# Two of ten weighted row sums move from VectorE to ScalarE and TensorE in the last stage of a decoder layer

## Chip, core and metric

The kernel runs on one NeuronCore of a Trainium2 chip. The metric is the device time of one execution in microseconds (us); less is better. A core has five engines that run their own instruction streams and meet only at semaphores: TensorE (PE, matmuls, into the accumulator memory PSUM), VectorE (DVE), ScalarE (ACT), GpSimd (POOL, here above all the issuer of indirect DMAs) and SyncE (SP, the issuer of most other DMAs).

## The reference, cut to what matters

The reference computes one decoder layer for 512 prompt tokens and 8 sample tokens of width 1024: a mixer of two attention groups, a mixture of experts with two experts for each token, and a final norm. The change lies behind the last expert, in the sum over the two experts, the residual and the norm:

```python
combine = jnp.sum(jax.nn.one_hot(expert_id, N_EXPERTS) * (g_w * top_w)[..., None], axis=1)
act = jax.nn.silu(gate) * up * combine[..., None]
y = jnp.einsum('nef,efd->nd', act, w_down)
x = x + y
output = rms_norm(x, norm_final)
```

Each token has two nonzero weights in `combine`, so its `y` is (first weight x the row of its first choice) + (second weight x the row of its second choice).

## The kernel before, in words

**Tiles.** The 520 tokens are five tiles: tiles 0 to 3 have 128 prompt rows each, tile 4 (the sample rows) has 8. `x[:, i, :]` holds tile i in SBUF, 1024 float32 to a row.

**Experts.** Sixteen experts run one after the other; the program streams their weights from memory. An expert's result rows are stored to `expert_rows` (`y_dram`) in memory. The last two experts (numbers 14 and 15, `LATE = 14`) are not stored: their rows stay in SBUF as `y_late`, and TensorE distributes them with 0/weight matrices `late_pick` (built earlier) straight into PSUM.

**The final stage.** After the stores have landed, POOL gathers, for each tile in the order `SUM_ORDER = (0, 4, 1, 2, 3)`, the two rows of each token from `expert_rows` (L2351, ten indirect DMAs). A tile then goes through these steps:

1. TensorE opens its two PSUM banks with zeros (`open_banks`, a bf16 product with zero weights, L2698). Tiles 0 and 4 are opened before the last down projection, tiles 1 and 2 right after it. Tile 3 uses tile 0's banks, and so is opened once tile 0 has been read for the last time.
2. VectorE, `add_rows(i)`: L2673 adds first weight x first rows to `x`; L2677 writes second weight x second rows + `x` into the banks.
3. TensorE adds the rows of the late experts with four matmuls of 64 rows by 512 columns (L2914), two on array rows 0 to 63 and two on 64 to 127.
4. ScalarE squares and sums the banks (L2452), then takes the inverse root by Ln and Exp (L2453, L2455).
5. VectorE, `scaled(i)`: L2683 multiplies the banks by that and by the gain, into `x`; SP stores `x` (L2309).

Each engine's order is written out by hand and is kept: VectorE does `add_rows` for 0, 4, 1, 2, then `scaled(0)`, `add_rows(3)`, then `scaled` for 4, 1, 2, 3. TensorE and ScalarE go through the tiles in `SUM_ORDER`. An `overflow` branch, ahead of the final stage on every engine, handles experts with more rows than were planned for; it is not entered with these inputs, but each engine loads a count and branches past it.

Of the kernel before, what the change touches and what calls it, by code (L numbers as in the profile page):

```python
# [16 lines left out]
ACT = mybir.ActivationFunctionType  # L17
# [19 lines left out]
TILES = QT + 1  # L37
# [30 lines left out]
FIRST = P + 2  # L68
SUM_ORDER = (0, 4, 1, 2, 3)
OPEN_FIRST = (0, 4)  # L70
CHUNKS = [("gate", 0), ("gate", 1), ("up", 0), ("up", 1), ("down", 0), ("down", 1), ("gate", 2), ("up", 2)]
CHUNKS += [("down", 2), ("gate", 3), ("up", 3)]
CHUNKS += [(w, j - (w == "down")) for j in range(4, 15) for w in ("gate", "up", "down")]
# [118 lines left out]
def body(nc, ctx, a, out, cf_at, cf_n, cb_at, cb_n):  # L192
# [1969 lines left out]
    for i in SUM_ORDER:  # L2162
        sg.mark(f"gathered{i}", i, 32)
        sg.mark("early", ("first", i))
        sg.mark("early", i)
    for i in OPEN_FIRST + (1, 2):
        sg.mark("late_full", ("open", i))
    for i in SUM_ORDER:
        if i == 2:
            sg.mark("late_full", ("open", 3))  # L2170
        sg.mark("late_full", i)
        sg.mark("ssq_final", i)
        sg.mark("final", i)
        sg.mark("st_y", i, 16)
    final_waits = [(n, t) for n, t in sg.total.items() if n.startswith("st_")]
# [68 lines left out]
    def expert_sync(sp, kind, key):  # L2244
        if kind == "expert0":
            sg.wait(sp, "x_full", ("vproj", LATE_VALUES[-1]))
            load_chunk(sp, 0, FIXED[0])
            load_chunk(sp, 1, FIXED[1])
        elif kind == "chunk":
            n, = key  # L2250
            if n == 3:
                sg.wait(sp, "z_full", sb_units[-1])
            elif n == 4:
                sg.wait(sp, "t_full", ("probT",) + turned[-1] + (1,))
            elif n == 2:
                sg.wait(sp, "pv", turned[-1])
                sp.wait_ge(sg["st_v"], sg.total["st_v"])
            elif n == 5:
                sg.wait(sp, "m_full", ("wout", QT - 1, 1))
            elif n == 6:  # L2260
                sg.wait(sp, "m_full", ("wout", QT - 1, 3))
            load_chunk(sp, n, FIXED[CHUNKS[n][1]])
        elif kind == "chunk_part":
            n, part = key
            if part == 0:
                sg.wait(sp, "squares", QT - 1)
                load_chunk(sp, n, FIXED[CHUNKS[n][1]], (slice(0, 4), slice(6, 8)))
            else:
                sp.wait_ge(sg["e_rowsT_full"], 2)
                sp.wait_ge(sg["st_h2"], sg.total["st_h2"])  # L2270
                load_chunk(sp, n, FIXED[CHUNKS[n][1]], (slice(4, 6),))
        elif kind == "experts":
            expert_reg = list(FIXED)

            def next_expert(j):

                expert_reg.append(sp.value_load(order_i[0:1, j:j + 1], min_val=0, max_val=NE - 1))

            for n in range(RING, len(CHUNKS)):
                before, j = USED[n - RING]  # L2280
                if CHUNKS[n] == ("gate", 3):
                    sg.wait(sp, "x_dve", ("order",))
                if CHUNKS[n][0] == "gate":
                    next_expert(CHUNKS[n][1])
                sp.wait_ge(sg["e_" + before], freed(j))
                load_chunk(sp, n, expert_reg[CHUNKS[n][1]])
                if CHUNKS[n] == ("gate", LATE - 1):
                    sg.wait(sp, "x_dve", ("idx",))
                    sg.wait(sp, "extra", 0)
                    sg.wait(sp, "y_slots", 0)  # L2290
                    sp.dma_start(gain[:, :], a["norm_final"].rearrange("(o d) -> o d", o=1).partition_broadcast(P).rearrange(
                        "p o d -> p (o d)")).then_inc(sg["gain_in"], 16)
            def more(v):
                e = sp.value_load(extra_i[0:1, bass.ds(v, 1)], min_val=0, max_val=NE - 1)
                row = sp.value_load(extra_i[0:1, bass.ds(v + EXTRA, 1)], min_val=0, max_val=NE * CAP - P)
                load_all(sp, e, sg["v_w"])
                sp.dma_start(more_f[:, :], table[bass.ds(row, P), :]).then_inc(sg["v_idx"], 16)
                sp.wait_ge(sg["v_y"], 2 * v + 2)
                sp.dma_start(y_dram[bass.ds(v * P + EXPERT_ROWS, P), :], y_more).then_inc(sg["v_st"], 16)
                sp.wait_ge(sg["v_st"], 16 * v + 16)  # L2300
                sp.sem_inc(sg["v_passed_sp"], 1)

            sp.wait_ge(sg["e_down"], finished(LAST))
            overflow(sp, more, lambda: sp.sem_inc(sg["v_all"], 1))
        elif kind == "final":
            for i in SUM_ORDER:
                sg.wait(sp, "final", i)
                dst = out["y_p"][0, i * P:(i + 1) * P, :] if i < QT else out["y_s"][:, 0, :]
                sp.dma_start(dst, x[0:ROWS[i], i, :]).then_inc(sg["st_y"], 16)  # L2309

    def expert_gps(pool, kind, key):
# [10 lines left out]
        elif kind == "experts":  # L2322
# [32 lines left out]
            def gather_more():  # L2355
                pool.wait_ge(sg["v_all"], 2)
                for i in range(TILES):
                    for k in range(2):
                        nc.gpsimd.indirect_dma_start(gathered_more[0:ROWS[i], 2 * i + k, :], None, y_dram,
                                                     bass.IndirectOffsetOnAxis(ap=more_slots[0:ROWS[i], i, k:k + 1], axis=0)  # L2360
                                                     ).then_inc(sg["v_gathered"], 16)

            pool.wait_ge(sg["e_rowsT_full"], 2 * LAST)
            overflow(pool, more, gather_more)
    def expert_act(act, link, inverse_rms, kind, key):
# [10 lines left out]
        elif kind == "experts":  # L2376
# [68 lines left out]
                A.copy(y_more[:, 0:512], bank[2][:, :]).then_inc(sg["v_y"], 1)  # L2445
            overflow(act, more)
        elif kind == "final":
            for i in SUM_ORDER:
                r = ROWS[i]
                junk = work[0:r, 2048:3072].rearrange("p (a b) -> p a b", a=2)  # L2450
                sg.wait(act, "late_full", i)
                link(A.activation(junk, final_banks(i), ACT.Square, accum_out=small[0:r, 16 + i:17 + i]))  # L2452
                link(A.activation(small[0:r, 16 + i:17 + i], small[0:r, 16 + i:17 + i], ACT.Ln, bias=c["eps"][0:r],  # L2453
                                  scale=1.0 / D))
                A.activation(small[0:r, 16 + i:17 + i], small[0:r, 16 + i:17 + i], ACT.Exp, scale=-0.5  # L2455
                             ).then_inc(sg["ssq_final"], 1)

    def expert_dve(dve, link, kind, key):
        V = nc.vector
# [26 lines left out]
        elif kind == "experts":  # L2486
# [85 lines left out]
            def add_more():  # L2572
                dve.wait_ge(sg["v_gathered"], 32 * TILES)
                for i in range(TILES):
                    r, xi = ROWS[i], x[0:ROWS[i], i, :]
                    for k in range(2):
                        link(V.scalar_tensor_tensor(xi, gathered_more[0:r, 2 * i + k, :], weight[0:r, i, k:k + 1], xi,
                                                    ALU.mult, ALU.add))
                V.memset(smi[:, 40:41], 0).then_inc(sg["v_added"], 1)

            def y_out(j):
                if UNITS[j] <= 64:
# [86 lines left out]
        elif kind == "final":  # L2669
            def add_rows(i):  # L2670
                r, xi, to = ROWS[i], x[0:ROWS[i], i, :], final_banks(i)
                sg.wait(dve, f"gathered{i}", i)
                V.scalar_tensor_tensor(xi, gathered_rows(i, 0), weight[0:r, i, 0:1], xi, ALU.mult, ALU.add  # L2673
                                       ).then_inc(sg["early"], 1)
                sg.wait(dve, "early", ("first", i))
                sg.wait(dve, "late_full", ("open", i))
                V.scalar_tensor_tensor(to, gathered_rows(i, 1).rearrange("p (a b) -> p a b", a=2), weight[0:r, i, 1:2],  # L2677
                                       xi.rearrange("p (a b) -> p a b", a=2), ALU.mult, ALU.add).then_inc(sg["early"], 1)

            def scaled(i):  # L2680
                r = ROWS[i]
                sg.wait(dve, "ssq_final", i)
                V.scalar_tensor_tensor(x[0:r, i, :].rearrange("p (a b) -> p a b", a=2), final_banks(i), small[0:r, 16 + i:17 + i],  # L2683
                                       gain[0:r, :].rearrange("p (a b) -> p a b", a=2), ALU.mult, ALU.mult
                                       ).then_inc(sg["final"], 1)

            for i in (0, QT, 1, 2):
                add_rows(i)
            sg.wait(dve, "gain_in", "final")
            scaled(0)  # L2690
            add_rows(3)
            for i in (QT, 1, 2, 3):
                scaled(i)
# [21 lines left out]
    def expert_pe(pe, kind, key):  # L2715
# [186 lines left out]
        elif kind == "final":  # L2902
# [3 lines left out]
            for i in SUM_ORDER:  # L2906
                to = final_banks(i)
                if i == 2:
                    sg.wait(pe, "final", 0)
                    open_banks(3).then_inc(sg["late_full"], 1)  # L2910
                sg.wait(pe, "early", i)
                for q in range(2):
                    for h in range(2):
                        ins = T.matmul(to[:, h, :], late_pick(q, i)[64 * h:64 * h + 64, :], y_late[q][64 * h:64 * h + 64, :],  # L2914
# [368 lines left out]
```

## Time and profile before

| | us |
|---|---|
| median of 3 runs | 756.84 (755.36 to 759.11) |
| profiled execution, own time | 751.01 |
| its span | 749.2 |
| TensorE busy in the span | 697.4 (93%) |
| VectorE busy | 343.3 (46%) |
| ScalarE busy | 216.3 (29%) |
| first indirect gather of the final stage issued | 719.05 |
| end of VectorE's last instruction (744.78 + 1.28) | 746.06 |

The span is what the profiler saw of one execution; the execution's own time is 1.8 us more. The runs that make the median were timed without the profiler and are 0.6 to 1.1% above the profiled one. Times of instructions are counted from the span's start. An engine's busy share over the whole span says little about the last 20 us, which is all that the change touches.

### The profile page before, as it was taken

Reading aid. Unit: us, or ns where it says so; the run is one execution under the profiler, and the core shown is the slowest. Engines: PE = TensorE matmul, PEld = TensorE weight load, DVE = VectorE, ACT = ScalarE, POOL = GpSimd, SP = SyncE. Lnnn points to the kernel's source line nnn. Section 1 sums busy time; section 2 is a strip of 40 time slices with the busy share of each in tenths; the row PEclk is TensorE's granted clock in tenths of the full one; section 3 lists DMA queues with packets and bytes.
Section 4 is the critical chain, followed back from the end, with each engine's and each line's share of the span. In section 5 each row is a group of like instructions: output and inputs, shape, how many; then the busy total and the mean of one; then the engine's idle time right before and its main releaser. Section 6 shows DMA issues by size and latency. Waiting matters only on the chain.

```text
span 749.2 us, 13606 instructions
## 1 busy us (share of the span) xinstructions
PE 697.4 (93%) x5261; PEld 382.9 (51%) x5261; DVE 343.3 (46%) x770; ACT 216.3 (29%) x557; POOL 125.5 (17%) x174
## 2 busy tenths in 40 slices
PE   7978999999999989989979999989899999999985
PEld 3445456444554444545545564744465565566531
DVE  6422103595222465664784665523823543322238
ACT  1111111112321555757757852001101101101114
POOL 0111000120000443252242242110100000000040
PEclk9999999999999999989999999999999999999999
DMA  8266890677658530000000059999999999999995
GB/s 278 88 179 179 250 387 24 239 239 234 210 170 219 217 145 1 1 4 1 1 29 1 6 190 372 305 379 400 363 363 375 399 408 397 396 401 400 413 348 206
DMA packets 101523, 172.55 MB, mean 230 GB/s; under 512 B 22925, under 2 KB 40685, under 8 KB 101426
## 3 DMA queue, kind: packets, MB, share of 16 engines
q1 hardware_dynamic: 79714, 142.83, 53.6%
q10 hardware_dynamic: 18656, 20.35, 8.1%
q0 software_dynamic: 3088, 8.49, 3.2%
q8 instruction: 43, 0.70, 0.4%
q14 instruction: 22, 0.18, 0.1%
HBM read 151.78 MB, written 22.98 MB: 233 GB/s over the span
## 4 chain that ended last, share of the span: by engine, by line
PE 71%; DVE 7%; SPq 6%; issue 6%; ACT 4%; DMA 4%; POOL 0%; ACTq 0%; DVEq 0%
PE bank L2752 15%; PE bank L3242 13%; PE bank L2008 7%; PE bank L3225 6%; PE bank L2781 6%; SPq L1191 4%; PE bank L1946 3%; PE bank L1925 3%; PE bank L1804 2%; PE bank L2711 2%; PE bank L1959 2%; PE bank L2742 2%; DMA pages<-page_table 2%; PE bank L3246 1%; PE bank L2060 1%
## 5 line engine op out<-in xcount | busy, mean ns | idle before, releaser
L3242 PE MATMUL bank<-reg 128*128 128x512 f32 (+1 forms) x352 | 146.8, 562 | 1.2 <-DMA reg<-w_in 0.8
L2752 PE MATMUL bank<-reg,qreg 128*32 128x128 f32 (+2 forms) x1072 | 100.1, 340 | 0.9 <-ACT qreg L2380 0.6
L3242 PEld LDWEIGHTS bank<-reg 128*128 128x128 f32 x352 | 64.2, 191 | 59.4 <-issue 55.8
L2752 PEld LDWEIGHTS bank<-reg,qreg 128*32 128x32 f32 (+2 forms) x1072 | 59.3, 126 | 39.6 <-issue 25.1
L1290 POOL TENSOR_SCALAR reg<-reg,st,gates 128x128 f32<-128x128 f32 (+3 forms) x64 | 41.3, 655 | 181.9 <-DVE st L1578 181.8
L3225 PE MATMUL bank<-cf,reg 128*128 128x128 f32 (+1 forms) x384 | 61.4, 278 | 9.4 <-DVE rt L1769 4.9
L2008 PE MATMUL bank<-reg 128*128 128x512 f32 x128 | 65.0, 632 | 0.4 <-DVE x L1690 0.3
L3225 PEld LDWEIGHTS bank<-cf,reg 128*128 128x128 f32 (+1 forms) x384 | 41.6, 141 | 29.3 <-issue 24.5
L3076 ACT ACTIVATE work<-bank 128x128 f32<-128x128 f32 (+5 forms) x107 | 40.8, 411 | 49.0 <-PE bank L3225 47.7
L1574 DVE TENSOR_REDUCE st<-bank 128x2 f32<-128x256 f32 (+3 forms) x32 | 26.3, 823 | 44.8 <-PE bank L1927 44.7
L2781 PE MATMUL bank<-reg,work 128*32 128x256 f32 (+1 forms) x336 | 44.2, 475 | 1.8 <-ACT work L2391 1.6
L3180 DVE COPY work<-bank 128x128 f32<-128x128 f32 (+4 forms) x55 | 22.8, 429 | 50.4 <-PE bank L3225 50.3
L2330 POOL DMA_INDIRECT work<-h_rows,ids x14 | 13.6, 969 | 180.7 <-PE bank L2800 128.0
L1405 ACT ACTIVATE reg<-bank,st 128x128 f32<-128x128 f32 (+3 forms) x64 | 33.2, 525 | 27.4 <-DVE st L1574 27.1
L3043 POOL TENSOR_TENSOR reg<-reg,cf 128x128 f32<-128x128 f32 (+5 forms) x30 | 15.4, 532 | 145.7 <-ACT reg L3133 135.1
L1946 PE MATMUL bank<-work,vreg 128*64 128x128 f32 x480 | 37.1, 284 | 2.0 <-DVE work L3180 2.0
L1946 PEld LDWEIGHTS bank<-work,vreg 128*64 128x64 f32 x480 | 25.4, 137 | 24.4 <-issue 21.9
L2498 DVE TENSOR_SCALAR work<-work 128x256 f32<-128x256 f32 (+3 forms) x16 | 5.4, 335 | 70.8 <-ACT work L2386 70.7
L2499 DVE RECIPROCAL work<-work 128x256 f32<-128x256 f32 (+3 forms) x16 | 36.0, 2253 | 0.6
L2008 PEld LDWEIGHTS bank<-reg 128*128 128x128 f32 x128 | 22.8, 199 | 17.0 <-issue 16.1
L2399 ACT COPY work<-bank 128x512 f32<-128x512 f32 (+1 forms) x16 | 9.0, 560 | 72.5 <-PE bank L2781 52.1
L3133 ACT COPY reg<-bank 128x512 f32<-128x512 f32 (+1 forms) x20 | 10.9, 547 | 62.4 <-PE bank L3242 62.4
(380 smaller groups left out, 944.5 us busy)
## 6 DMA issues: line engine op xcount, KB each, us to landing
reg<-w_down SPq DMA_DIRECT2D x13, 2048.0 KB, 19.6
reg<-w_gate SPq DMA_DIRECT2D x12, 2048.0 KB, 13.6
reg<-w_up SPq DMA_DIRECT2D x10, 2048.0 KB, 16.0
reg<-w_in ACTq DMA_DIRECT2D x16, 512.0 KB, 6.0
expert_rows<-vreg SPq DMA_DIRECT2D x14, 512.0 KB, 6.7
vreg<-w_up SPq DMA_DIRECT2D x3, 2048.0 KB, 12.8
reg<-cache_sb_k SPq DMA_DIRECT2D x16, 256.0 KB, 4.4
reg<-cache_sb_v SPq DMA_DIRECT2D x16, 256.0 KB, 4.1
```

What stands on the lines that cost most here:

```text
L1191: sp.dma_start(dst[64 * pg:64 * pg + 64, l], src[:, l]).then_inc(sg[f"pair{q % PAIRS}"], 16)
L1290: ins = G.tensor_scalar(prob, prob, w[:, e:e + 1], gate[:, e:e + 1], ALU.mult, ALU.mult)
L1405: nc.scalar.activation(prob_of(key, e)[:, 0:n], at(ring, key)[:, 0:n], ACT.Exp, bias=st[:, top:top + 1], accum_out=st[:, col:col + 1]).the ...
L1574: V.tensor_reduce(st[:, top:top + 2], psum[:, 2:4, 0:n], AX.X, ALU.max, negate=True).then_inc(sg["arg"], 1)
L1946: ins = T.matmul(to[64 * e:64 * e + 64, :], v, probT[:, turn_at[key] % 3, e, k * P:(k + 1) * P], start=(k == 0 and b != WIN), stop=(k == i ...
L2008: ins = T.matmul(at(ring, ("wout", i, group))[0:r, :], chunks_of(i)[:, part, 0:r], w_out[group // 2][:, k, 512 * half:512 * half + 512], s ...
L2499: link_loop(V.reciprocal(s_, s_), 3 * j + 2)
L2752: ins = T.matmul(to[rows, at_:at_ + w], rowsT[b][:, k, r0:r0 + n], w_[:, k, h * w:(h + 1) * w], start=(k == 0), stop=(k == KD - 1))
L2781: ins = T.matmul(to[rows, at_:at_ + w], actsT[j % 2][:, 4 * r0 // P + k % per, a0:a0 + n], w_[:, k, w * h:w * h + w], start=(k == 0), stop ...
L3076: ins = nc.scalar.activation(dst, src, ACT.Copy, scale=scale)
L3225: ins = nc.tensor.transpose(dst, src, ident[0:src.shape[0], 0:src.shape[0]])
L3242: ins = nc.tensor.matmul(at("m", ("proj", n))[:, 0:w], hT[:, k, i * P:(i + 1) * P], win[:, pos % 2, k, 0:w], start=(k == 0), stop=(k == KD ...
```

## The change

`ON_ACT = (4, 1)`: for the sample rows and for tile 1, VectorE's second instruction of `add_rows` is left out. In its place ScalarE, in a new function `second(i)`, writes second weight x second rows into the opened banks. `x` (with the first choice's rows added by VectorE, as before) is added by TensorE: two matmuls with the identity as the stationary operand and 512 columns of `x` as the moving one, ahead of the four with the late rows. ScalarE does `second(4)` ahead of its first square and `second(1)` behind tile 0's norm; TensorE waits for it through `ssq_final`. Inside the overflow branch, gathers are repeated and waits added; the branch is not entered.

```diff
+ON_ACT = (4, 1)
...
+            def second(i):
+                sg.wait(act, f"gathered{i}", i)
+                sg.wait(act, "late_full", ("open", i))
+                A.activation(final_banks(i), gathered_rows(i, 1).rearrange("p (a b) -> p a b", a=2), ACT.Copy,
+                             scale=weight[0:ROWS[i], i, 1:2]).then_inc(sg["ssq_final"], 1)
+
+            second(4)
             for i in SUM_ORDER:
...
                 A.activation(small[0:r, 16 + i:17 + i], small[0:r, 16 + i:17 + i], ACT.Exp, scale=-0.5
                              ).then_inc(sg["ssq_final"], 1)
+                if i == 0:
+                    second(1)
...
                 V.scalar_tensor_tensor(xi, gathered_rows(i, 0), weight[0:r, i, 0:1], xi, ALU.mult, ALU.add
                                        ).then_inc(sg["early"], 1)
+                if i in ON_ACT:
+                    return
...
-                sg.wait(pe, "early", i)
+                if i in ON_ACT:
+                    sg.wait(pe, "early", ("first", i))
+                    sg.wait(pe, "ssq_final", ("second", i))
+                    for h in range(2):
+                        T.matmul(to[:, h, :], ident[0:ROWS[i], 0:ROWS[i]], x[0:ROWS[i], i, 512 * h:512 * h + 512],
+                                 start=False, stop=False)
+                else:
+                    sg.wait(pe, "early", i)
                 for q in range(2):
```

VectorE's stream in the final stage, from its start to `add_rows(3)`, before the change (`bank` is PSUM, `reg` and `vreg` hold gathered rows; what stands in brackets are the semaphores waited on):

```order
L2673 SCALAR_TENSOR_TENSOR x<-reg,weight,x 128x1024 [waits gathered0]
L2677 SCALAR_TENSOR_TENSOR bank<-reg,weight,x 128x1024 [waits late_full,early]
L2673 SCALAR_TENSOR_TENSOR x<-vreg,weight,x 8x1024 [waits gathered4]
L2677 SCALAR_TENSOR_TENSOR bank<-vreg,weight,x 8x1024 [waits late_full,early]
L2673 SCALAR_TENSOR_TENSOR x<-reg,weight,x 128x1024 [waits gathered1]
L2677 SCALAR_TENSOR_TENSOR bank<-reg,weight,x 128x1024 [waits late_full,early]
L2673 SCALAR_TENSOR_TENSOR x<-reg,weight,x 128x1024 [waits gathered2]
L2677 SCALAR_TENSOR_TENSOR bank<-reg,weight,x 128x1024 [waits late_full,early]
L2683 SCALAR_TENSOR_TENSOR x<-bank,small,gain 128x1024 [waits ssq_final,gain_in]
```

And of the changed kernel (L2699 is the old L2673, L2705 the old L2677, L2711 the old L2683):

```order
L2699 SCALAR_TENSOR_TENSOR x<-reg,weight,x 128x1024 [waits gathered0]
L2705 SCALAR_TENSOR_TENSOR bank<-reg,weight,x 128x1024 [waits late_full,early]
L2699 SCALAR_TENSOR_TENSOR x<-vreg,weight,x 8x1024 [waits gathered4]
L2699 SCALAR_TENSOR_TENSOR x<-reg,weight,x 128x1024 [waits gathered1]
L2699 SCALAR_TENSOR_TENSOR x<-reg,weight,x 128x1024 [waits gathered2]
L2705 SCALAR_TENSOR_TENSOR bank<-reg,weight,x 128x1024 [waits late_full,early]
L2711 SCALAR_TENSOR_TENSOR x<-bank,small,gain 128x1024 [waits ssq_final,gain_in]
```

Two of the bank writes are gone, so tile 2's gathered rows are asked for two instructions earlier.

TensorE's stream from tile 0's late rows to the opening of tile 3's banks, before (`work,cf` and `work,vreg` are the late rows with their two `late_pick` matrices):

```order
L2914 MATMUL bank<-work,cf 128x512 [waits early]
L2914 MATMUL bank<-work,cf 128x512
L2914 MATMUL bank<-work,vreg 128x512 x2
L2914 MATMUL bank<-work,cf 8x512 [waits early]
L2914 MATMUL bank<-work,cf 8x512
L2914 MATMUL bank<-work,vreg 8x512 x2
L2914 MATMUL bank<-work,cf 128x512 [waits early]
L2914 MATMUL bank<-work,cf 128x512
L2914 MATMUL bank<-work,vreg 128x512 x2
L2698 MATMUL bank<-cb,wr 128x512 [waits final]
```

And of the changed kernel, where L2943 is the new identity product, L2949 the old L2914 and L2726 the old L2698:

```order
L2949 MATMUL bank<-work,cf 128x512 [waits early]
L2949 MATMUL bank<-work,cf 128x512
L2949 MATMUL bank<-work,vreg 128x512 x2
L2943 MATMUL bank<-x,cf 8x512 [waits ssq_final,early]
L2943 MATMUL bank<-x,cf 8x512
L2949 MATMUL bank<-work,cf 8x512 x2
L2949 MATMUL bank<-work,vreg 8x512 x2
L2943 MATMUL bank<-x,cf 128x512 [waits ssq_final,early]
L2943 MATMUL bank<-x,cf 128x512
L2949 MATMUL bank<-work,cf 128x512 x2
L2949 MATMUL bank<-work,vreg 128x512 x2
L2726 MATMUL bank<-cb,wr 128x512 [waits final]
```

Two pairs of identity products have come in, ahead of everything that tiles 1, 3 and 2 need of TensorE.

ScalarE's stream from the end of the overflow branch, in the changed kernel, where L2467 is `second(i)` and L2475 to L2478 are the old L2452 to L2455; before, these rows stood there without the two of L2467:

```order
L2467 ACTIVATE bank<-vreg,weight 8x1024 [waits late_full,gathered4]
L2475 ACTIVATE work,small<-bank 128x1024 [waits late_full]
L2476 ACTIVATE small<-small,cf 128x1 [waits act_chain]
L2478 ACTIVATE small<-small 128x1 [waits act_chain]
L2467 ACTIVATE bank<-reg,weight 128x1024 [waits late_full,gathered1]
L2475 ACTIVATE work,small<-bank 8x1024 [waits late_full]
```

The sample rows' write stands ahead of tile 0's square, tile 1's behind tile 0's norm.

## Rows read from the trace of the kernel before

**Rows 1.** The page, busy time of each engine over the span

```profile
PE 697.4 (93%) x5261; PEld 382.9 (51%) x5261; DVE 343.3 (46%) x770; ACT 216.3 (29%) x557; POOL 125.5 (17%) x174
```

**Rows 2.** Chain of waits that ended last: start us, us, what

```profile
727.14 1.30 DVE x L2673
...
734.67 1.29 DVE x L2673
735.96 0.02 issue
735.98 0.04 DVE bank L2677
736.01 1.17 issue
737.18 1.29 DVE x L2683
738.47 0.05 issue
738.52 0.60 PE bank L2698 x2
739.12 3.93 PE bank L2914 x16
743.05 0.02 issue
743.07 1.12 ACT work L2452 x2
...
744.78 1.28 DVE x L2683
```

**Rows 3.** Timeline, DVE: start, us, operation, [idle before <-releaser]

```profile
727.14 1.28 DVE L2673 SCALAR_TENSOR_TENSOR x<-reg,weight,x 128x1024 f32<-128x1024 f32 x1 [3.28 <-DMA reg<-expert_rows,y_slots]
...
730.96 1.28 DVE L2677 SCALAR_TENSOR_TENSOR bank<-vreg,weight,x 8x1024 f32<-8x1024 f32 x1
732.16 1.27 DVE L2673 SCALAR_TENSOR_TENSOR x<-reg,weight,x 128x1024 f32<-128x1024 f32 x1
```

**Rows 4.** Timeline, PE; one row holds four records, two to a matmul

```profile
716.98 2.33 PE L2698 MATMUL bank<-cb,wr 32*128 32x512 bf16 x10
730.00 1.03 PE L2698 MATMUL bank<-cb,wr 32*128 32x512 bf16 x4 [0.68 <-ACT work L2399]
730.96 1.13 PE L2914 MATMUL bank<-work,cf 64*128 64x512 f32 x4
731.92 1.02 PE L2914 MATMUL bank<-work,vreg 64*128 64x512 f32 x4
732.88 1.03 PE L2914 MATMUL bank<-work,cf 64*8 64x512 f32 x4
733.74 1.02 PE L2914 MATMUL bank<-work,vreg 64*8 64x512 f32 x4
739.05 1.13 PE L2914 MATMUL bank<-work,cf 64*128 64x512 f32 x4
741.04 1.13 PE L2914 MATMUL bank<-work,cf 64*128 64x512 f32 x4
```

**Rows 5.** Groups by line and shape: busy us, mean ns

```profile
L2752 PE MATMUL bank<-reg,qreg 128*128 128x512 f32 x80 | 35.2, 595 | 0.0
L2698 PE MATMUL bank<-cb,wr 32*128 32x512 bf16 x18 | 4.6, 376 | 2.4 <-DVE x L2683 1.7 <-ACT work L2399 0.7
L1391 ACT ACTIVATE reg<-reg 128x1024 f32<-128x1024 f32 x4 | 4.2, 1058 | 0.0
```

**Rows 6.** Timeline, ACT

```profile
729.36 0.59 ACT L2399 COPY work<-bank 128x512 f32<-128x512 f32 x1 [4.60 <-PE bank L2781]
732.99 1.02 ACT L2452 ACTIVATE work<-bank 128x1024 f32<-128x1024 f32 x1 [3.05 <-PE bank L2914]
734.47 0.20 ACT L2455 ACTIVATE small<-small 128x1 f32<-128x1 f32 x1
```

**Rows 7.** Tile 2's second gather: its row, and its time to landing

```profile
727.74 1.50 POOL L2351 DMA_INDIRECT reg<-expert_rows,y_slots x1 [0.30 <-issue]
DMA to landing us min/median/max: 6.3/6.3/6.3
```

**Rows 8.** Stretches: us, busy of each engine, granted clock, DMA

```profile
736.00:740.00 4.00, 2.28 (x10) 0.60 (x8) 3.96 (x4) 2.05 (x6) 0.00 (x0) 1.00 0.17 69
388.00:392.00 4.00, 2.40 (x6) 1.43 (x7) 3.79 (x5) 3.28 (x8) 0.57 (x1) 0.71 0.00 0
```

More of the change, by code:

```diff
@@ L2164, in body @@
         sg.mark("early", ("first", i))
-        sg.mark("early", i)
+        if i not in ON_ACT:
+            sg.mark("early", i)
     for i in OPEN_FIRST + (1, 2):
@@ L2171, in body @@
         sg.mark("late_full", i)
+        if i == 0:
+            sg.mark("ssq_final", ("second", 4))
         sg.mark("ssq_final", i)
+        if i == 0:
+            sg.mark("ssq_final", ("second", 1))
         sg.mark("final", i)
@@ L2303, in expert_sync, with rows_landed @@
             sp.wait_ge(sg["e_down"], finished(LAST))
-            overflow(sp, more, lambda: sp.sem_inc(sg["v_all"], 1))
+            def rows_landed():
+                for i in SUM_ORDER:
+                    sg.wait(sp, f"gathered{i}", i)
+            overflow(sp, more, lambda: sp.sem_inc(sg["v_all"], 1), rows_landed)
         elif kind == "final":
@@ L2360, in gather_more @@
                                                      bass.IndirectOffsetOnAxis(ap=more_slots[0:ROWS[i], i, k:k + 1], axis=0)
+                                                     ).then_inc(sg["v_gathered"], 16)
+                pool.wait_ge(sg["v_added"], 1)
+                for i in SUM_ORDER:
+                    for k in range(2):
+                        nc.gpsimd.indirect_dma_start(gathered_rows(i, k), None, y_dram,
+                                                     bass.IndirectOffsetOnAxis(ap=y_slots[0:ROWS[i], i, k:k + 1], axis=0)
                                                      ).then_inc(sg["v_gathered"], 16)
@@ L2456, in expert_act @@
                              ).then_inc(sg["ssq_final"], 1)
+                if i == 0:
+                    second(1)
     def expert_dve(dve, link, kind, key):
@@ L2579, in add_more @@
                 V.memset(smi[:, 40:41], 0).then_inc(sg["v_added"], 1)
+                dve.wait_ge(sg["v_gathered"], 64 * TILES)
             def y_out(j):
```

## The prediction, made before the changed kernel ran

> **What bounds the kernel now.** The page's shares [rows 1] say that TensorE is the busy engine of the span, 93%, and VectorE is busy for 46%. That is an average over the whole layer, and the change touches only what follows the last gathers, so I went to the chain of waits over the last 60 us [rows 2], and then to the timeline of the last 35 us engine by engine. The reader is to see two parts there. From 727.14 to 738.47 the chain is VectorE's: it runs one 1.25 us instruction after the other, nine of them, and its row at 730.96, for instance, is followed at 732.16 with no idle time [rows 3]. From 738.52 to 743.05 the chain is TensorE's: it opens tile 3's banks and adds the late rows of tiles 2 and 3 [rows 2]. Then come one square and norm on ScalarE (743.07 to 744.78) and the last scaling on VectorE, to 746.06; the rest of the span, 3.1 us, is the last store. So in this stage VectorE bounds the first half, but the handover at 738.5 matters: TensorE there waits for `scaled(0)` alone, having been idle since the late rows of tile 1. Work taken from VectorE moves the end only if TensorE reaches tile 3's opening earlier than 738.52, and this change gives TensorE more to do ahead of just that point.
>
> **What is removed.** Two bank writes of VectorE, 1.25 us each from start to start (730.96 to 732.16 is 1.20, others 1.3) [rows 3], 2.5 us. Not all of it is worth having: VectorE next wants tile 2's gathered rows. Before it reached them at 734.67. Now it would after `first(0)`, `second(0)`, `first(4)` and `first(1)`, the last ending about 732.2; but the second gather of tile 2 was issued at 727.74 and takes 6.3 us, so it lands at 734.04 [rows 7]. VectorE gains 734.67 - 734.04 = 0.63 us and idles 1.8 us. If nothing else held it, its eight instructions after the first one of tile 2 put the last scaling at 734.04 + 8 x 1.25 = 744.04 instead of 744.78: the change cannot give more than 0.7 us, whatever the rest costs.
>
> **What is added on ScalarE.** Two activations of 1024 columns from SBUF. None writes to PSUM in this trace; the nearest row, SBUF to SBUF with 128x1024, is 1.06 us [rows 5], and I take that. ScalarE ends its last copy at 729.95, and its first square starts at 732.99 [rows 6], released by TensorE. Between them stands the overflow branch. TensorE gets past its own branch between its last down matmul and 730.00, where it was waiting for ScalarE's copy, with 0.68 us idle [rows 4], so the branch is worth 0.7 us at most there. I take the same for ScalarE: `second(4)` runs 730.65 to 731.7, beside TensorE's tile 0 (730.96 to 732.88), which hides it, with 1.2 us to spare. If the cover were gone, because ScalarE's branch takes all of its 3.05 us, `second(4)` would run 733.0 to 734.05 and TensorE's tile 4 would start 1.17 us later; that is the upper bound. `second(1)` starts when tile 0's Exp ends, 734.67 [rows 6], and ends at 735.75. TensorE needs it later than that, as the next sum shows, so it costs nothing. A price of twice 1.06 would make TensorE wait 0.3 us there.
>
> **What is added on TensorE.** Two matmuls with 512 float32 columns for each of the two tiles. A matmul of this kind leaves two records. The full-array row has 80 records in 35.2 us, 0.44 each [rows 5], so tile 1's pair, four records, costs 1.76 us. The pairs of L2914 are cheaper only because two lie side by side on different array rows: four records take 730.96 to 731.92, 0.96 us, or 0.86 with 8 output columns (732.88 to 733.74) [rows 4]. The identity products of a tile share their array rows, 0 to 127 or 0 to 7, so I price them one after the other: 1.76 us for tile 1, and 2 x 0.86 = 1.72 for the sample rows, where being 8 rows small saves nothing, since the columns that stream through are 512 all the same. The lower bound is full overlap, 0.96 and 0.86.
>
> There is also a change of array shape at each entry to and exit from the identities. Ten zero matmuls in a row take 2.33 us [rows 4], and one record lasts 0.376 [rows 5], so their starts are (2.33 - 0.376) / 9 = 0.217 us apart. The four of 730.00 are followed at 730.96 by L2914 [rows 4]: 0.96, where four steps are 0.87. So a change of shape costs about 0.1 us. Four more of them make 0.4. The Trainium skill, page "TensorEngine Tiling (Array Packing)", section "Key Properties", states that a switch of tiling mode drains TensorE; it gives no time. The trace agrees in sign, with 0.1 us, and by that rule taken as no cost at all the sum would be 0.4 less.
>
> **The sum, on TensorE, which never waits in it:**
> - tile 0's late rows end at 732.88, as before [rows 4];
> - tile 4: 1.72 identities + 1.72 late rows (2 x 0.86) + 0.2 shapes: 736.52. `second(1)` was done at 735.75;
> - tile 1: 1.76 + 1.92 (2 x 0.96) + 0.2: 740.40;
> - tile 3's opening, 0.53 (738.52 to 739.05 [rows 2, 4]): 740.93. `scaled(0)`, for which it waits, is done near 737.8, no longer in the way;
> - tile 2's late rows, 1.92: 742.85. VectorE writes tile 3's banks meanwhile, 741.0 to 742.3;
> - tile 3's late rows until ScalarE's square starts: 741.04 to 743.07 was 2.03 [rows 2, 4]: 744.88.
>
> The square started at 743.07, so it is 1.8 us late. Behind it nothing is in the way: VectorE has `scaled(4)`, `(1)` and `(2)` to do between 742.3 and 746.1, and tile 3's norm is ready at 744.88 + 1.71 = 746.6. The last scaling and store are unchanged. The end moves by +1.8 us, 749.2 to 751.0 for the span and 751.01 to 752.8 for the profiled execution. That execution is 5.8 us under the median of the runs shown, so I put the difference on the median: 756.84 + 1.8 = 758.6.
>
> What stays: gathers, stores, weights and all before 729.95 are untouched, and the code in the branch isn't run. Store traffic is no denser than before.
>
> **Rivals.**
> - *The relief pays.* For it: the chain is VectorE's for 11 us, and the Trainium skill, page "Perfetto Trace Analysis", section "Optimizing Scalar/DVE Operations", says that with VectorE saturated, moving work to ScalarE may make sense. Against: the landing at 734.04, and TensorE in order. It needs the identities to overlap in pairs. Then tile 4 ends at 732.88 + 0.86 + 1.72 = 735.46, tile 1 runs from `second(1)`'s end, 735.75, to 735.75 + 0.96 + 1.92 = 738.63, and the same steps lead to 738.63 + 0.53 + 1.92 + 2.03 = 743.11: no change. With identities at nothing, VectorE's bound of -0.7 us holds. So -0.7 to 0, 756.1 to 756.8. Chance 0.08.
> - *ScalarE arrives late with the sample rows* (slower still). One instruction, `second(4)`, ahead of tile 0's square and tile 4's matmuls; it decides from an end later than 732.88. Price up to 1.17 us on top, so +1.8 to +3.0: 758.6 to 759.8. Against it stands the 0.7 us of TensorE's branch. Chance 0.14.
> - *TensorE's clock falls to its lower level, 1.2 GHz* (slower by more than can be missed). The granted clock was 1.00 in 736 to 740 in which TensorE was busy for 2.28 us, and 0.71, so partly at the lower level, in 388 to 392, where it was busy for 2.40 [rows 8]; idle time of that size can thus go either way. With more matmuls in the tail the changed kernel idles less, which speaks against. If it fell at 732.88, the 12.0 us of stream above would double: 758.6 + 12.0 = 770.6. Chance 0.03.
> - *Something outside this sum*, code that lies otherwise in memory and is fetched at another time, by 2 to 4 us either way: 0.03.
>
> **How the numbers follow.** The forecast itself, +1.4 (shapes free) to +2.3, has 0.72. What can be told from no change here is about 0.5%, 3.8 us, since three runs of one kernel spread over 3.75 us. Forecast and first two rivals all lie within that; what makes a verdict of slower are the spread on top of 1.8 to 3.0 us, the clock, and half of the last case: 0.10. Faster needs the first rival and a lucky spread: 0.03. The range: the lowest case 756.1 less the spread of a median, 1.6, gives 754.5; the highest of the second rival, 759.8, plus 2.2 gives 762.
>
> **What the profile of the changed kernel would show.** Right: TensorE has no idle time from 730.96 to the late rows of tile 3; each identity pair takes 1.7 to 1.8 us; VectorE idles 1.8 us before tile 2's first rows and again before it writes tile 3's banks; ScalarE's square of tile 3 starts 12.0 us after tile 4's first matmul (it was 10.2); the chain names TensorE from 732.9 on. Wrong: identities at 0.9 us a pair; TensorE waiting for ScalarE's L2467 at tile 4; chain still VectorE's; or any difference ahead of 729.

## The result: 0.5% slower in the first comparison, and the profile after

Before 756.34 us (median of 21 runs), the changed kernel 759.83 (21 runs); ratio 1.0053, 95% interval 1.0034 to 1.0071. In microseconds that is +4.0 (2.6 to 5.4); forecast was +1.8, which lies under that interval, though the 759.83 itself lies within the forecast range of 754.5 to 762. A second comparison, later and under other conditions, gave 1.0014 (0.9997 to 1.0030). That the two differ turned out to be the main thing to learn here.

The profiled execution of the changed kernel has a span of 755.9 us, against 749.2. Its busy times by engine, which answer to [rows 1]:

```profile
PE 704.0 (93%) x5269; PEld 385.5 (51%) x5269; DVE 340.7 (45%) x768; ACT 218.2 (29%) x559; POOL 126.4 (17%) x174
```

The end of its chain of waits (start us, us, what), which answers to [rows 2]. L2780 is the last up product, L2949 the late rows, L2943 the identities, L2726 the openings:

```profile
699.25 21.91 DMA reg<-w_up
721.20 5.36 PE bank L2780 x32
726.56 2.06 issue
...
735.23 1.03 PE bank L2726 x4
736.27 1.92 PE bank L2949 x8
738.18 1.81 PE bank L2943 x4
739.99 1.82 PE bank L2949 x8
741.81 1.91 PE bank L2943 x4
743.72 1.92 PE bank L2949 x8
745.64 0.53 PE bank L2726 x2
746.17 3.66 PE bank L2949 x16
749.85 1.12 ACT work L2475 x2
```

From 736.27 to 749.83 the chain is TensorE's alone, with no gap. VectorE, which held it for 11 us in [rows 2], has no part in that stretch. What ScalarE and VectorE do there, from the timeline (start, us, operation, [idle before <-releaser]), which answers to [rows 3, 6]:

```profile
735.61 1.11 ACT L2467 ACTIVATE bank<-vreg,weight 8x1024 f32<-8x1024 f32 x1 [0.43 <-issue]
...
739.81 1.10 ACT L2467 ACTIVATE bank<-reg,weight 128x1024 f32<-128x1024 f32 x1
...
740.01 1.28 DVE L2711 SCALAR_TENSOR_TENSOR x<-bank,small,gain 128x1024 f32<-128x1024 f32 x1 [2.10 <-ACT small L2478]
...
746.28 1.29 DVE L2705 SCALAR_TENSOR_TENSOR bank<-reg,weight,x 128x1024 f32<-128x1024 f32 x1 [3.80 <-PE bank L2726]
```

VectorE has been relieved of 2.5 us and now idles 2.10 and 3.80 us.

Three numbers, read from the timelines, order everything that follows. **S** goes from TensorE's first late-row matmul of tile 0 to ScalarE's square of tile 3; behind that square every trace has the same 6.1 us. Before: 743.07 - 730.96 = 12.11 [rows 2, 4]. After: 749.85 - 736.20 = 13.65. **G** goes from POOL's first gather of the stage to that same first matmul; it says how late TensorE is against the gathers. Before: 730.96 - 719.05 = 11.9. After: 736.20 - 720.33 = 15.9. **L** goes from VectorE's first weighted sum (tile 0's L2673, now L2699) to that matmul; it says how far VectorE is ahead, which G does not where VectorE itself starts late. Before: 730.96 - 727.14 = 3.82. After: 736.20 - 729.70 = 6.50. So of the 6.7 us between the two spans, S explains 1.5. The other 5.2 lie ahead of tile 0's late rows, where no matmul or weighted sum was changed, 4.0 of them in G.

G's part begins with the last up product. Stretches of both kernels from its first matmul to VectorE's product with it (length, busy of PE, PEld, DVE, ACT, POOL, granted clock, DMA share, GB/s), before:

```profile
719.60:723.40 3.80, 3.67 (x32) 2.21 (x32) 0.00 (x0) 0.00 (x0) 2.88 (x4) 1.00 0.96 363
```

and after:

```profile
721.20:728.10 6.90, 5.36 (x32) 2.97 (x32) 0.00 (x0) 0.00 (x0) 5.07 (x7) 0.75 0.81 277
```

The same 32 records take 3.67 us at a granted clock of 1.00, and 5.36 at 0.75, partly at the lower level of 1.2 GHz. That is 1.7 of G's 4.0 us. Another 1.5 lie right behind it: VectorE's product with the result, for which TensorE waits, started 0.12 us after the last record before and 1.59 us after it now:

```profile
723.43 0.42 DVE L2506 TENSOR_TENSOR work<-work,bank 128x256 f32<-128x256 f32 x1 [7.24 <-PE bank L2752]
```

```profile
728.15 0.42 DVE L2531 TENSOR_TENSOR work<-work,bank 128x256 f32<-128x256 f32 x1 [10.53 <-PE bank L2780]
```

None of this code was changed. Either the changed kernel causes it, or the first profile of before was an execution in which it happened not to occur.

### The profile page after: what moved, and what is told of

Same layout as the page of the kernel before. It is cut to its first block, busy times and chain, and to the rows that moved or that the text cites. A ratio compares the mean times of both kernels' runs of the same rounds, so it can differ in the third digit from the quotient of the medians.

```text
span 755.9 us, 13624 instructions
## 1 busy us (share of the span) xinstructions
PE 704.0 (93%) x5269; PEld 385.5 (51%) x5269; DVE 340.7 (45%) x768; ACT 218.2 (29%) x559; POOL 126.4 (17%) x174
## 4 chain that ended last, share of the span: by engine, by line
PE 74%; issue 8%; DVE 6%; ACT 4%; DMA 3%; another core or an unknown queue 2%; POOL 1%; SPq 0%; DVEq 0%; ACTq 0%; POOLq 0%
PE bank L2780 15%; PE bank L3277 14%; PE bank L2009 7%; PE bank L2809 6%; PE bank L3260 6%; PE bank L1947 3%; PE bank L1926 3%; DMA reg<-w_up 3%; PE bank L1805 2%; PE bank L1960 2%; PE bank L2770 2%; PE bank L2949 1%; PE bank L3281 1%; PE bank L2061 1%
## 5 line engine op out<-in xcount | busy, mean ns | idle before, releaser
L3277 PE MATMUL bank<-reg 128*128 128x512 f32 (+1 forms) x352 | 148.8, 569 | 0.8 <-DVE reg L3212 0.4
L2780 PE MATMUL bank<-reg,qreg 128*32 128x128 f32 (+2 forms) x1072 | 101.8, 344 | 1.1 <-ACT qreg L2396 0.6
L2780 PEld LDWEIGHTS bank<-reg,qreg 128*32 128x32 f32 (+2 forms) x1072 | 60.0, 128 | 40.7 <-issue 26.6
L2009 PE MATMUL bank<-reg 128*128 128x512 f32 x128 | 62.7, 613 | 0.4 <-DVE x L1691 0.3
L3260 PEld LDWEIGHTS bank<-cf,reg 128*128 128x128 f32 (+1 forms) x384 | 42.2, 142 | 28.9 <-issue 24.3
L2009 PEld LDWEIGHTS bank<-reg 128*128 128x128 f32 x128 | 22.0, 192 | 16.7 <-issue 15.8
L2809 PEld LDWEIGHTS bank<-reg,work 128*32 128x32 f32 (+1 forms) x336 | 15.7, 123 | 27.6 <-issue 22.7
```

What stands on the lines that cost most here:

```text
L2009: ins = T.matmul(at(ring, ("wout", i, group))[0:r, :], chunks_of(i)[:, part, 0:r], w_out[group // 2][:, k, 512 * half:512 * half + 512], s ...
L2780: ins = T.matmul(to[rows, at_:at_ + w], rowsT[b][:, k, r0:r0 + n], w_[:, k, h * w:(h + 1) * w], start=(k == 0), stop=(k == KD - 1))
L2809: ins = T.matmul(to[rows, at_:at_ + w], actsT[j % 2][:, 4 * r0 // P + k % per, a0:a0 + n], w_[:, k, w * h:w * h + w], start=(k == 0), stop ...
L3260: ins = nc.tensor.transpose(dst, src, ident[0:src.shape[0], 0:src.shape[0]])
L3277: ins = nc.tensor.matmul(at("m", ("proj", n))[:, 0:w], hT[:, k, i * P:(i + 1) * P], win[:, pos % 2, k, 0:w], start=(k == 0), stop=(k == KD ...
```

## Experiments

### A second profile of before, the branch's code alone, and TensorE 2.2 us later

`before_again` is the kernel before, unchanged.

> The kernel before, unchanged, for a second profile. Two numbers are read from it: G, from the first indirect gather of the last stage to TensorE's first late-row matmul of tile 0 (11.9 us in the first profile of before, 15.9 in the changed kernel's), and S, from that matmul to the square of tile 3 (12.1 before, 13.65 after). Theory A (the last weights' landing decides G, it varies from run to run, and the kernel before takes up to 2.1 us of lateness beside VectorE's work): S falls as G grows, S = 12.1 at G = 11.9, down to 10.05 at G of 14 or more. Rival B (the loss is a constant one, S does not depend on G): S = 12.1 whatever G is.

`branch_only` keeps of the change what stands in the overflow branch:

```diff
-ON_ACT = (4, 1)
+ON_ACT = ()
```

> The changed kernel with no tile given to ScalarE: only the code in the overflow branch is left of the change. Theory A: the branch's code costs nothing, ratio to before 1.000 within 0.002, S as in the kernel before at the same G. Rival C (code that lies otherwise in memory is fetched at another time, so most of the 4.0 us comes from ahead of the last stage): ratio 1.003 or more.

`before_late` and `after_late` get ten zero matmuls behind the last transposes, ahead of the last down projection:

```diff
             pe.wait_ge(sg["picked"], TILES)
+            for _ in range(5):
+                zero_banks(0, True, True)
             for i in OPEN_FIRST:
```

> The kernel before with ten more zero matmuls on TensorE (2.2 us) ahead of the last down projection, nothing else changed. Theory A: VectorE's chain runs on meanwhile, so the end moves by 2.2 us less the slack that TensorE has there, which is 2.1 us where the weights landed early and 0 where they landed late: +0.1 to +2.2 us, S falls to between 10.0 and 12.1, G is 2.2 us more. Rival B: +2.2 us, ratio 1.003, and S stays 12.1.

> The changed kernel with the same ten zero matmuls (2.2 us) on TensorE. Theory A: TensorE is the bound from there to the end, all of it is paid, +2.2 us over the changed kernel, so ratio to before 1.005 + 0.003 = 1.008, and S stays 13.65 at any G. If VectorE or ScalarE bounded the changed kernel, the end would move by less than 2.2 and S would shrink.

Measured, ratios to before, whose runs on the same chip had a median of 754.98: `branch_only` 1.0004 (0.9986 to 1.0022), so no cost of the code in the branch shows. `before_late` 1.0027 (1.0003 to 1.0052). `after_late` 1.0078 (1.0064 to 1.0093). Each pays, as far as the intervals tell, the 2.2 us that were added. For the kernel before the best value, 2.0 us, speaks against its first profile, where 2.1 us of slack stood, but its interval, 0.2 to 3.9 us, is too wide to decide. The medians of the two late kernels are 4.2 us apart.

The profile of `branch_only`, whose final stage is that of before, shows why. TensorE and ScalarE there:

```profile
735.77 1.03 PE L2727 MATMUL bank<-cb,wr 32*128 32x512 bf16 x4 [0.69 <-ACT work L2415]
736.73 1.13 PE L2950 MATMUL bank<-work,cf 64*128 64x512 f32 x4
...
740.47 1.13 PE L2950 MATMUL bank<-work,cf 64*128 64x512 f32 x4
741.43 1.02 PE L2950 MATMUL bank<-work,vreg 64*128 64x512 f32 x4
742.38 0.60 PE L2727 MATMUL bank<-cb,wr 32*128 32x512 bf16 x2
...
742.91 1.13 PE L2950 MATMUL bank<-work,cf 64*128 64x512 f32 x4
...
746.66 1.02 ACT L2476 ACTIVATE work<-bank 128x1024 f32<-128x1024 f32 x1
```

Tile 3's opening (742.38) follows tile 1's late rows at once; in [rows 2] it waited for VectorE until 738.52. S is 746.66 - 736.73 = 9.93, with G = 18.6 and L = 7.9. TensorE came late, VectorE had used the time to get ahead, and TensorE bounds the stage in the old order as well. Against this S the change costs 13.65 - 9.93 = 3.72 us: both identity pairs in full.

`before_again` did not come out as expected: G = 15.8, yet S = 13.64. Theory A wanted 10. Two mishaps stand in its timeline. VectorE lost 2.1 us ahead of its second instruction:

```profile
730.13 1.28 DVE L2673 SCALAR_TENSOR_TENSOR x<-reg,weight,x 128x1024 f32<-128x1024 f32 x1 [1.14 <-issue]
...
733.50 1.29 DVE L2677 SCALAR_TENSOR_TENSOR bank<-reg,weight,x 128x1024 f32<-128x1024 f32 x1 [2.09 <-remote]
...
745.05 1.73 PE L2914 MATMUL bank<-work,vreg 64*128 64x512 f32 x4
...
746.57 1.92 PE L2914 MATMUL bank<-work,cf 64*128 64x512 f32 x4
```

The profile names as releaser only "remote", another core or a queue that it doesn't know. The DMA view of 732.4 to 733.2 has one packet of an instruction queue:

```profile
q14 instruction: 1, 0.01, 3.1%
```

So a fetch of instructions runs just ahead of 733.50; in the first profile there was room for it while VectorE waited for the gathers [rows 3]. That the fetch is the cause is inferred from this order, not tested. `branch_only` has the same order (1.44 us, packet at 731.2), but one trace speaks against it: in `after_late` the same VectorE instruction waited for 3.18 us, to 731.54, and this queue's packet lies at 726.0 to 726.5, ahead of that wait. The second mishap are the last two rows above: 1.73 and 1.92 us for what takes 1.02 and 1.13 in [rows 4]. The clock had fallen, in a stretch that follows TensorE's wait for `scaled(0)`, which was 1.72 us as in the first profile, where the clock stayed at 1.00:

```profile
745.00:750.00 5.00, 4.49 (x14) 1.52 (x10) 4.67 (x4) 2.07 (x5) 0.00 (x0) 0.66 0.34 123
```

My third rival, the clock falling in the tail, thus exists, but in the kernel before; in the changed kernel TensorE does not pause there. Neither constant S (rival B) nor S by G alone (theory A) holds for before.

S by L does. Where VectorE bounds the old order, L + S is one constant, the length of VectorE's work: 15.93 in the first profile and 15.94 and 15.93 in the two `before_dense` profiles below. So S is 15.93 - L, down to TensorE's own 9.93, which is reached at L = 6.0. For `before_again`, with L = 5.77, that gives 10.16; the 2.09 us that VectorE lost and 1.4 us for the slow matmuls (745.05 to 749.54 is 4.49, where 740.01 to 743.07 was 3.06) bring it to 13.7, against 13.64 measured.

### One pair, and no pair

`only_sample` has `ON_ACT = (4,)`. `no_identity` is the changed kernel without the identity matmuls, so it leaves `x` out of the sums of those two tiles:

```diff
-                    for h in range(2):
-                        T.matmul(to[:, h, :], ident[0:ROWS[i], 0:ROWS[i]], x[0:ROWS[i], i, 512 * h:512 * h + 512],
-                                 start=False, stop=False)
```

> Only the sample rows are given to ScalarE; tile 1 is as before. Theory D (in most executions TensorE, not VectorE, bounds the kernel before from tile 0's late rows on, S = 9.9, because the last up product runs at the lower clock; each identity pair is then paid in full): one pair, 1.8 us, S = 11.7, ratio to before 1.0024. The prediction's sum (VectorE bounds the kernel before, S = 12.1): -0.1 us, ratio 1.000.

> The changed kernel without the four identity matmuls, so x is not added for the sample rows and tile 1; all else is as in the changed kernel. Theory D: 3.7 us of the change go, but tile 1 still waits for ScalarE's second write, which ends 1.05 us after tile 0's Exp: TensorE idles 1.1 us there, S = 11.1, +1.1 us over before, ratio 1.0015. The prediction's sum: VectorE's bound, -0.7 us, ratio 0.999. If ScalarE's writes were the cost: ratio stays near 1.005.

Measured, before at 755.93: `only_sample` 1.0005 (0.9982 to 1.0028), `no_identity` 1.0015 (0.9993 to 1.0038). The interval of `only_sample` holds both theories' ratios, 1.0024 and 1.000. That of `no_identity` holds theory D's 1.0015, barely excludes the prediction's sum (0.999), and excludes the 1.005 that ScalarE's writes would cost if they were the cause. The traces decide more: S = 11.74 with one pair (forecast 11.7) and 11.07 with none (forecast 11.1). Without identities TensorE waits for ScalarE's second write of tile 1, in the timeline of `no_identity`:

```profile
742.13 1.13 PE L2946 MATMUL bank<-work,cf 64*128 64x512 f32 x4 [1.06 <-ACT bank L2467]
```

That wait is hidden behind the sample rows' identities in the changed kernel. ScalarE's detour alone would cost 1.1 us in the late alignment, even if adding x were free.

### What makes TensorE late: zero matmuls and dense ones

TensorE waits for the last up weights with ten zero matmuls (L2698 at 716.98 [rows 4]). Ten more of them:

```diff
-            for _ in range(5):
+            for _ in range(10):
                 zero_banks(0, True, True)
             gate_or_up(LAST, 1, sg["e_up"])
```

> The kernel before with ten instead of five pairs of zero matmuls ahead of the last up product, while TensorE waits for that product's weights (2.2 us more, beside a wait of 1.0 to 1.1 us). Theory D: TensorE is kept busy up to the weights, the granted clock stays at the upper level, the up product and what follows it take 3.8 us up to VectorE's product instead of 7.3 to 8.0, at the price of up to 1.2 us; G falls from 16 or more to 12.5 to 13, the end comes 2 to 3 us earlier, ratio 0.996 to 0.997, and S is above 11 with VectorE the bound. If the clock doesn't depend on that idle time: +1.1 us, ratio 1.0015.

> The changed kernel with the same five pairs more. Theory D: G falls as in before_zeros, S stays 13.65, so the end is 13.65 less that kernel's S later than before_zeros: +1.5 to +2.0 us and no longer +3.7; ratio to before near 0.999 to 1.000. If the change costs the same 3.7 us wherever TensorE stands, it is 3.7 us over before_zeros.

Measured: 1.0068 (1.0043 to 1.0093) and 1.0131 (1.0098 to 1.0163). My expectation was wrong in sign: instead of holding the clock, the longer row of zeros lowered it further. `before_zeros`, from the zeros' start, then from the up product's, then from VectorE's product:

```profile
717.80:723.30 5.50, 5.50 (x24) 1.96 (x22) 0.00 (x0) 0.59 (x1) 2.82 (x3) 0.80 0.95 368
723.30:734.00 10.70, 5.95 (x33) 3.21 (x32) 0.00 (x0) 0.00 (x0) 6.56 (x7) 0.66 0.87 286
734.00:742.00 8.00, 7.47 (x20) 2.05 (x22) 6.64 (x6) 0.37 (x1) 0.00 (x0) 0.52 0.28 112
```

TensorE is busy for all of the first stretch and the clock falls nonetheless. The Trainium skill, page "TensorE: Matmul & The Clock Gate", section "What's actually happening", says that activity releases the throttle; in this row TensorE was busy with zero matmuls without a gap, and the granted clock was 0.80. G became 24.8 in both kernels, S is 9.94 and 13.66, and the medians are 5.1 us apart.

The clock is not all of that 24.8. From 729.25 TensorE waited 5.28 us for VectorE's product, which started 4.80 us after the up product's last record:

```profile
734.05 0.42 DVE L2506 TENSOR_TENSOR work<-work,bank 128x256 f32<-128x256 f32 x1 [17.00 <-remote]
734.53 0.69 PE L2758 MATMUL bank<-cf,work 128*128 128x128 f32 x2 [5.28 <-DVE work L2506]
```

In eight of the nine profiles in which the up product ran at a lower clock, this start was late too, by 1.1 to 4.9 us; in the ninth, `after_again` below, and in all five others it came 0.12 us after the last record. What held VectorE is not known: in `before_zeros` no instruction packet lies between 729.3 and 734.1.

So the zeros were replaced by four dense float32 matmuls (3.7 us), whose result is overwritten:

```diff
-            for _ in range(5):
-                zero_banks(0, True, True)
+            for n in range(4):
+                T.matmul(bank[6 + n % 2][:, :], x[:, 3, 0:P], x[:, 3, 512:D], start=True, stop=True)
```

> The kernel before, but in place of the ten zero matmuls that TensorE issues while it waits for the last up product's weights (2.2 us), four full-array float32 matmuls of x by x (3.5 us) into the same two banks, whose result is overwritten. [...] Theory E (the clock falls because the array is next to idle there, zeros or none): with dense matmuls it stays at the upper level, the up product to VectorE's product takes 3.8 us instead of 7.0 to 8.0, G falls to 12 to 13, the end comes 2 to 4 us earlier, ratio 0.995 to 0.997, S between 11 and 14 with VectorE the bound. If the clock is lost for another reason: no gain, G 16 or more, ratio 1.000 to 1.002.

> The changed kernel with the same four dense matmuls. With the last product at the upper clock, TensorE reaches tile 0 early, and VectorE bounds the kernel before as in its first profile. Theory D then wants S = 13.65 here and a difference to before_dense of 1.0 to 2.0 us (13.65 less that kernel's S), instead of the 3.7 us where TensorE bounds both. If the change costs 3.7 us over before_dense too, the alignment doesn't matter. If the clock doesn't hold: 3.7 us over before_dense.

In this comparison before was at 749.72, with a mean clock of 0.981 instead of 0.975. `before_dense` 1.0006 (0.9986 to 1.0025), `after_dense` 1.0030 (1.0012 to 1.0048). The clock held, in `before_dense` from the dense matmuls on:

```profile
715.40:719.00 3.60, 3.60 (x10) 1.43 (x8) 0.00 (x0) 0.59 (x1) 1.39 (x2) 1.00 0.95 385
719.00:723.50 4.50, 3.90 (x35) 2.41 (x34) 0.42 (x1) 0.00 (x0) 3.28 (x5) 1.00 0.84 311
```

In all three profiles with dense matmuls the clock from 719.0 to 723.5 is 1.00; of the eleven with zeros it is 1.00 in two and 0.62 to 0.84 in nine. All three dense ones come from comparisons in which the runs of before average 0.981, though; the one profile with zeros from there, `after_again` below, has 0.76. The forecast gain of 2 to 4 us did not come. The difference between the two dense kernels did come as forecast: 751.61 - 749.65 = 1.96 us, with S = 11.66 and 13.65, so 1.99; that the medians agree so closely is luck, since the two intervals overlap. With TensorE on time, VectorE bounds the old order, and by S the change costs about half of what it costs otherwise.

### The changed kernel and the dense matmuls once more

> The changed kernel once more, on whatever chip it gets. The runs of before differ by chip in time and in mean granted clock: 755 to 756 us at 0.975 on two chips, 749.7 us at 0.981 on a third. Theory D (the change costs 13.65 less the S of before, and that S is 9.9 where the last up product runs at the lower clock and 11.7 to 12.1 where it doesn't): on a chip whose runs of before are at 0.975, ratio 1.004 to 1.005 (3.7 us and less); on one at 0.981, ratio 1.002 to 1.003 (1.5 to 2.0 us). If the cost doesn't depend on the chip's clock: 1.0053 as in the first comparison, on either.

> The kernel before with the four dense matmuls in place of the zero ones, once more, on the same chip as the run above. Theory E: on a chip at 0.975, where the clock falls before the last up product, the dense matmuls hold it, ratio 0.995 to 0.998; on a chip at 0.981 there is little to hold, ratio 1.000 as on the chip before. If dense matmuls do nothing for the clock: 1.000 to 1.002 on both.

Before was at 749.35 here, mean clock 0.981. `after_again` 1.0014 (0.9997 to 1.0030): that holds 1.0024, the cost of 1.8 us, and excludes the 1.0053 of the first comparison. `before_dense2` 1.0009 (0.9994 to 1.0024), clock held, S = 11.25. Both ran on the chip on which before had 755.0 us at 0.975 earlier, so it is not the chip alone that differs.

All profiles, in microseconds:

| kernel | G | L | S |
|---|---|---|---|
| before, first profile | 11.9 | 3.82 | 12.11 |
| before_dense2 | 12.7 | 4.68 | 11.25 |
| before_dense | 13.1 | 4.28 | 11.66 |
| before_again (two mishaps) | 15.8 | 5.77 | 13.64 |
| branch_only | 18.6 | 7.91 | 9.93 |
| before_late, before_zeros | 24.3, 24.8 | 12.79, 8.99 | 9.94, 9.94 |
| only_sample | 15.9 | 5.82 | 11.74 |
| no_identity | 17.6 | 8.94 | 11.07 |
| after_dense, after_again | 12.7, 13.7 | 4.58, 5.06 | 13.65, 13.66 |
| changed kernel, after_late | 15.9, 15.9 | 6.50, 7.53 | 13.65, 13.66 |
| after_zeros | 24.8 | 8.95 | 13.66 |

The G of the two late kernels is not set by the 2.2 us alone: the traced execution of `before_late` was the slowest of its twelve, that of `after_late` the fastest of its five.

The changed kernel's S is the same at any G and L: TensorE bounds it always. The old order's S falls from 12.1 to 9.9 as TensorE comes later against VectorE's start. The cost of the change is the difference, 1.5 to 2.4 us where TensorE is on time and 3.7 where L is 6.0 or more.

## Why the prediction was right, and where it fell short

- **What the relief is worth.** Right: VectorE's two instructions bought nothing. With early gathers it waits for the landing (1.62 us in `after_dense`, 1.69 in `after_again`; forecast 1.8), with late TensorE it waits for ScalarE and TensorE.
- **ScalarE's price.** 1.11 and 1.10 us, against 1.06 from an SBUF row. `second(4)` started 0.43 us behind the last copy (forecast at most 0.7) and ended before it was needed. The rival in which it arrives late did not occur.
- **TensorE's price.** 1.81 and 1.91 us for the pairs with a change of shape each, where I had 1.82 and 1.86; 1.82 and 1.92 for the late rows behind them, where I had 1.82 and 2.02. The sum from tile 4's first matmul to tile 3's square is 11.74 (738.11 to 749.85), against 12.0. The change in S against the profile it was made on is +1.54, against +1.8. The 8-row identities indeed cost as much as those of 128 rows. The rival with overlapping pairs is refuted.
- **What was mis-sized.** The first term of the sum on TensorE, "tile 0's late rows end at 732.88, as before", and the baseline that goes with it, "From 727.14 to 738.47 the chain is VectorE's": they took the alignment of one profile for that of the runs, and the list of signs named this itself ("any difference ahead of 729"): the changed kernel's last down product starts at 730.04, against 725.66. `branch_only`, at 1.0004 (0.9986 to 1.0022), shows that the code in the branch is not the reason. That profile's execution, 751.01 us, was 5.8 us under the median, which I noted and then only added to the forecast. In it the clock held through the last up product (3.67 us) and VectorE's product came at once; in nine of eleven profiles with zero matmuls the up product took 5.3 to 6.0 us, and in eight of these VectorE's product came late besides. Where TensorE is late, the 2.2 us by which TensorE waited for VectorE in [rows 2] (12.11 - 9.93) are not there, and +1.5 becomes +3.7. That falls in the 4.0 (2.6 to 5.4) of the first comparison, and 1.5 doesn't; the second comparison (-0.2 to +2.2 us) holds 1.5 and not 3.7.
- **What stays open.** Of the comparisons' runs only one each has a trace, so the share of late executions in either is inferred from mean clock and time, and that this share makes the two comparisons differ is not shown. In the profiles of the changed kernel, `before_again` and `branch_only`, 2.06, 2.36 and 3.05 us lie between the up product's last record and TensorE's next matmul (0.59 in the first profile of before), because VectorE's product between them comes late; what holds VectorE there was not tried. The dense matmuls, which held the clock in their profiles, gained nothing against before. They were run only where the runs of before had a mean clock of 0.981, the same as their own, so there may have been little to gain; at 0.975 they were not run.

No version tried beats the kernel before.

## What to carry to other kernels

Moving work off the engine that the chain of waits names helps only as far as the next engine has room; lay out the receiving engine's stage as one sum, in its issue order, with the durations of its neighbours' rows, and see which comes first. Being small in rows did not make an identity pair cheap here: 1.81 us on 8 rows and 1.91 on 128, both over 1024 columns, each to save 1.25 on VectorE. And when the profiled execution is well under the median, ask which wait or clock fall it was spared, since the path in the median run may lead through another engine: here the cost of the change in the last stage goes from 1.5 to 3.7 us by that.

## What the runs showed of the hardware that was not expected

- Zero matmuls of 32 rows kept TensorE busy without holding its clock (0.80 over the zeros in `before_zeros`); with four dense float32 matmuls it was 1.00 in three profiles of three, all from comparisons in which before had 0.981.
- ScalarE wrote 1024 columns from SBUF to PSUM in 1.10 us, where SBUF to SBUF is 1.06 [rows 5] and PSUM to SBUF 1.02 [rows 6]. The Trainium skill, page "ScalarE: Activation LUTs", section "Step-by-step: what each stage is for", calls PSUM the faster destination for ScalarE; these rows, 1.10 against 1.06, do not agree.
- Behind the branch, which isn't entered, VectorE stalled at its second instruction with no releaser inside the program in four profiles: 2.09 us in `before_again`, 1.44 in `branch_only`, 0.74 in the changed kernel's and 3.18 in `after_late`. In the first two a packet of instruction queue q14 lies in the stall, in the third only at its end (731.7), in the last none.
- VectorE's product with the last up product's result started 0.12 us after TensorE's last record in six profiles and 1.1 to 4.9 us after it in eight, all eight with a granted clock under 1.00 in the up product.
